# Segment sums of a state-space mixer as two fp32r products, with the steps split into a high and a low part

## The reference

```python
cs = jnp.cumsum(dt * a.reshape(g, r), axis=2)
seg = cs[:, :, :, None] - cs[:, :, None, :]
decay_in = jnp.exp(jnp.where(lower, seg, -jnp.inf))
cb = jnp.einsum('bcqgn,bcsgn->bcqsg', cm, bm)
m = cb[..., None] * decay_in * dt[:, :, None]
y_diag = jnp.einsum('bcqsgr,bcsgrp->bcqgrp', m, x)
```

## Time and profile before

| | us |
|---|---|
| median of 3 runs | 3049.22 |
| lowest, highest | 3045.48, 3049.49 |
| the profiled execution | 3067.35 |
| its span, first to last instruction | 3065.7 |
| TensorE busy | 2827.2 (92%) |
| VectorE busy | 2144.5 (70%) |
| ScalarE busy | 1532.5 (50%) |
| GpSimd busy | 188.3 (6%) |
| mean granted TensorE clock | 0.962 of 2.4 GHz |

### The profile page before, as it was taken

The page is one execution under the profiler, slowest core; times in us unless marked ns, Lnnn a source line. Parts: engine busy times, 40 slices in busy tenths (PEclk is TensorE's granted clock), DMA queues, the critical chain, the costliest instruction groups (busy, mean ns, idle before and its releaser), DMA issues. The chain is left out here.

```text
span 3065.7 us, 50810 instructions
## 1 busy us (share of the span) xinstructions
PE 2827.2 (92%) x17878; PEld 2422.8 (79%) x17878; DVE 2144.5 (70%) x4117; ACT 1532.5 (50%) x2880; POOL 188.3 (6%) x180
## 2 busy tenths in 40 slices
PE   5999688899997993999999999999999999999993
PEld 4999455566665873999999999999999999999992
DVE  3565755666665448787788788788788778778773
ACT  4443444454444332565555555555655555555552
POOL 0000011011110001000000000000000000000001
PEclk8999888999999995999999999999999999999996
DMA  6111310121222434776787777677677677677754
GB/s 250 65 66 55 116 36 30 43 100 57 92 83 100 163 126 165 243 241 224 244 254 225 233 253 230 229 253 238 222 251 242 217 249 250 222 245 241 230 189 175
DMA packets 359718, 547.40 MB, mean 179 GB/s; under 512 B 14784, under 2 KB 287936, under 8 KB 359616
## 3 DMA queue, kind: packets, MB, share of 16 engines
q1 hardware_dynamic: 350720, 514.59, 49.2%
q0 software_dynamic: 8896, 31.46, 4.5%
HBM read 493.51 MB, written 52.49 MB: 178 GB/s over the span
## 5 line engine op out<-in xcount | busy, mean ns | idle before, releaser
L2578 PE MATMUL banks<-rowsT_parts,weights_high 128*128 128x384 f32 x4096 | 1184.7, 361 | 11.0 <-DVE hidden_parts L2507 7.1
L2579 PE MATMUL banks<-rowsT_parts,weights_low 128*128 128x192 f32 x4096 | 1026.4, 251 | 0.0
L2578 PEld LDWEIGHTS banks<-rowsT_parts,weights_high 128*128 128x128 f32 x4096 | 770.1, 188 | 19.9 <-DVE hidden_parts L2507 9.8
L2579 PEld LDWEIGHTS banks<-rowsT_parts,weights_low 128*128 128x128 f32 x4096 | 783.5, 191 | 1.4
L2444 DVE TENSOR_TENSOR weights_low<-keys_or_w_out,weights_high 128x1024 fp32r<-128x1024 f32 x512 | 603.0, 1216 | 1.4 <-ACT weights_high L2384 1.4
L2384 ACT ACTIVATE weights_high<-keys_or_w_out 128x1024 fp32r<-128x1024 f32 x512 | 523.8, 1049 | 39.6 <-PEq L2182 39.6
L2589 PE MATMUL banks<-weights_high,hidden_parts 128*128 128x512 f32 x1536 | 435.7, 392 | 0.0
L2494 DVE TENSOR_TENSOR h_or_keys_or_sums<-banks,h_or_keys_or_sums 128x192 f32<-128x192 f32 x512 | 181.2, 354 | 330.8 <-ACT h_or_keys_or_sums L2410 330.8
L2410 ACT ACTIVATE h_or_keys_or_sums<-banks 128x192 f32<-128x192 f32 x512 | 165.7, 324 | 460.2 <-PE banks L2579 456.4
L2589 PEld LDWEIGHTS banks<-weights_high,hidden_parts 128*128 128x128 f32 x1536 | 283.4, 188 | 69.8
L2589 PE MATMUL banks<-weights_low,hidden_parts 128*128 128x512 f32 (+1 forms) x1024 | 319.4, 393 | 0.0
(11 more groups left out here) (298 smaller groups left out, 3552.7 us busy)
## 6 DMA issues: line engine op xcount, KB each, us to landing
keys_or_w_out<-w_gate SPq DMA_DIRECT2D x128, 1024.0 KB, 5.1
keys_or_w_out<-w_up SPq DMA_DIRECT2D x128, 1024.0 KB, 6.8
slab_down<-w_down SPq DMA_DIRECT2D x128, 1024.0 KB, 4.8
arena_attend<-w_ada SPq DMA_DIRECT2D x8, 2048.0 KB, 7.5
arena_attend<-ssd_tiles SPq DMA_DIRECT2D x12, 992.0 KB, 9.0
arena_inputs<-w_ada SPq DMA_DIRECT2D x4, 2048.0 KB, 11.7
ssd_tiles<-arena_inputs SPq DMA_DIRECT2D x24, 256.0 KB, 2.0
mixed<-arena_attend SPq DMA_DIRECT2D x12, 512.0 KB, 2.9
```

Source lines behind the costliest of these rows:

```text
L2578: nc.tensor.matmul(out[:, 0:2 * CT], w_hi[:, u, block], x[:, k, :], start=k == 0, stop=False)
L2579: mm = nc.tensor.matmul(out[:, 0:CT], w_lo[:, u, block], x[:, k, 0:CT], start=False, stop=k == KD - 1)
```

## The change

Four things:

- The steps of a tile, `dta`, are split on VectorE (`steps`, new): `step_hi` is a cast to fp32r of [128, 16], `step_lo` the difference. This stands in slot h = 2 for the tile that follows, and in front of the first tile's spreads.
- `r_sum` has a part of each kind and is fp32r. VectorE makes both forward parts, [128, 8, 128] each, in slot h = 3, after the rotation; the spread in slot h = 6 goes. GpSimd makes both backward parts, and waits for `steps_done` in place of the tile's load.
- A segment product is two fp32r products into the same bank, with the triangles copied to fp32r once (`turns_r`).
- Places in the arena move to make room, and `eps_done` becomes part of `cleared`.

```diff
-    r_sum = A.at(A_R, 2, NS, P)
+    r_sum = core.once("decay_steps", [P, 2, 2, NS, P], F32R)
+    turns_r = core.once("triangles", [P, 2, P], F32R)
+    step_hi = core.once("steps_high", [P, 2, 16], F32R)
+    step_lo = core.once("steps_low", [P, 2, 16])
...
         def _(pool):
             def terms(g, j):
 
-                wait_apart(pool, tile_in[j], turn_of(g, j) + 16, pool_turns)
+                wait_apart(pool, steps_done, g + 1, pool_turns)
                 wait_apart(pool, seg_mm, g * 4, pool_turns)
-                nc.gpsimd.tensor_tensor(r_sum[:, 1], core.masks[:, M_GE, :].unsqueeze(1).broadcast_to([P, NS, P]),
-                                        dta[j][:, 8:16].unsqueeze(2).broadcast_to([P, NS, P]),
-                                        ALU.mult).then_inc(terms_b, 1)
+                for part, steps in enumerate((step_hi[:].bitcast(F32), step_lo[:])):
+                    ins = nc.gpsimd.tensor_tensor(r_sum[:, part, 1], core.masks[:, M_GE, :].unsqueeze(1).broadcast_to([P, NS, P]),
+                                                  steps[:, j, 8:16].unsqueeze(2).broadcast_to([P, NS, P]), ALU.mult)
+                ins.then_inc(terms_b, 1)
...
-            def terms(g, j):
+            def steps(g, j):
 
                 dve.wait_ge(tile_in[j], turn_of(g, j) + 16)
+                if not early(g):
+                    dve.wait_ge(terms_b, g - 1)
+                nc.vector.tensor_copy(step_hi[:, j], dta[j]).then_inc(steps_high, 1)
+                dve.wait_ge(steps_high, g + 3)
+                nc.vector.tensor_tensor(step_lo[:, j], dta[j], step_hi[:, j].bitcast(F32), ALU.subtract).then_inc(steps_done, 1)
+
+            def terms(g, j, part):
+                dve.wait_ge(steps_done, g + 1)
                 dve.wait_ge(seg_mm, g * 4)
-                nc.vector.tensor_tensor(r_sum[:, 0], core.masks[:, M_LE, :].unsqueeze(1).broadcast_to([P, NS, P]),
-                                        dta[j][:, 0:8].unsqueeze(2).broadcast_to([P, NS, P]),
-                                        ALU.mult).then_inc(terms_f, 1)
+                nc.vector.tensor_tensor(r_sum[:, part, 0], core.masks[:, M_LE, :].unsqueeze(1).broadcast_to([P, NS, P]),
+                                        (step_hi[:].bitcast(F32), step_lo[:])[part][:, j, 0:8].unsqueeze(2)
+                                        .broadcast_to([P, NS, P]), ALU.mult).then_inc(terms_f, 1)
...
+                    for d in range(2):
+                        nc.vector.tensor_copy(turns_r[:, d], core.masks[:, (M_GT, M_LT)[d], :]).then_inc(steps_high, 1)
                     keys_dve(dve, lambda t: front(t + 3, lo, 0, 0))
-                    terms(lo, 0)
+                    steps(lo, 0)
+                    for part in range(2):
+                        terms(lo, 0, part)
...
-                    if follows and h == 6:
-                        terms(g + 1, 1 - j)
...
                     if follows and h < 6:
                         front(h + 1, g + 1, place, 1 - j)
+                    if follows and h == 2:
+                        steps(g + 1, 1 - j)
+                    if follows and h == 3:
+                        for part in range(2):
+                            terms(g + 1, 1 - j, part)
...
             def seg(g, p, behind):
 
                 d, grp = divmod(p, 2)
-                pe.wait_ge((terms_f, terms_b)[d], g + 1)
+                pe.wait_ge((terms_f, terms_b)[d], g + 1 if d else g * 2 + 2)
                 if p:
                     pe.wait_ge(e_done, g * 4 + p)
                 elif behind is not None:
                     pe.wait_ge(y_mixed, behind + 1)
-                nc.tensor.matmul(b_y, core.masks[:, (M_GT, M_LT)[d], :],
-                                 r_sum[:, d, 4 * grp:4 * grp + 4, :].rearrange("p h q -> p (h q)"),
-                                 start=True, stop=True).then_inc(seg_mm, 1)
+                for part in range(2):
+                    mm = nc.tensor.matmul(b_y, turns_r[:, d, :],
+                                          r_sum[:, part, d, 4 * grp:4 * grp + 4, :].rearrange("p h q -> p (h q)"),
+                                          start=part == 0, stop=part == 1)
+                mm.then_inc(seg_mm, 1)
```

More of the change, by code:

```diff
@@ L181, in small, with once @@
         return self.stage.enter_context(self.nc.sbuf_tensor(name, shape, dtype))
-    def once(self, name, shape):
+    def once(self, name, shape, dtype=F32):
         if name not in self.kept:
-            self.kept[name] = self.small(name, shape)
+            self.kept[name] = self.small(name, shape, dtype)
         return self.kept[name]
@@ L228, in at @@
         return v.rearrange(f"p ({' '.join(names)}) -> p {' '.join(names)}", **dict(zip(names, dims)))
-ARENA = 48256
-A_NAT = 25984
-A_SLAB, A_MODT = 25984, 30080
+ARENA = 44032
+A_NAT = 24576
+A_SLAB, A_MODT = 24576, 28672
 SLABS = 4
@@ L334, in inputs @@
     heads = lambda t: t.rearrange("p (h e) -> p h e", h=NS)
-    consts_in, silu_c, cleared, eps_done = sem("consts_in"), sem("silu_c"), sem("mod_cleared"), sem("eps_set")
+    consts_in, silu_c, cleared = sem("consts_in"), sem("silu_c"), sem("eps_and_mod_cleared")
     slab_in = [sem(f"ada_slab_in{s}") for s in range(SLABS)]
@@ L624, in take_x @@
                     nc.scalar.activation(xnat[t], b_S1, ACT.Copy).then_inc(xnat_done, 1)
-            act.wait_ge(eps_done, 1)
+            act.wait_ge(cleared, 1)
             stats(0)
@@ L689, in _ @@
             nc.vector.memset(core.eps[:, 0:1], EPS)
-            nc.vector.memset(core.eps[:, 1:2], 1.0).then_inc(eps_done, 1)
+            nc.vector.memset(core.eps[:, 1:2], 1.0).then_inc(cleared, 1)
             nc.vector.memset(b_X[0][:, 0:P], 0.0)
@@ L1085, in _ @@
             pe.wait_ge(silu_c, 1)
-            pe.wait_ge(cleared, 1)
+            pe.wait_ge(cleared, 2)
             for s in range(SLABS):
@@ L1118, in _ @@
             chunk_state(NT - 1)
[L1121 to L1129, removed]
+A_KT, A_WUQ, A_V = 0, 8192, 9728
+A_P, A_PT = 13824, 15872
+A_KN, A_QN = 17920, 42496
+A_CN, A_CT2 = 19456, 20224
+A_MIXT = 20992
+A_OT, A_ROT = 23040, 23552
+A_QT, A_O = 28800, 30848
+A_E, A_XDT, A_Y, A_CBM = 32896, 34944, 35968, 38016
+A_REC, A_JUNKM = 38528, 24064
 A_KROT = A_NAT + NT * (NAT - QL)
@@ L1312, in mixers @@
         sem(n) for n in ("off_mm", "off_done", "diag_mm", "y_order", "y_gated", "y_sumsq", "y_rstd", "y_normed", "y_turned", "y_mixed"))
+    steps_high, steps_done = sem("triangles_and_steps_high"), sem("steps_split")
     pool_turns, dve_turns = sem("mix_pool_turns"), sem("mix_dve_turns")
@@ L1872, in first @@
                     pe.wait_ge(sem(name), hi)
+                if not r:
+                    pe.wait_ge(steps_high, 2)
                 scores(lo, 0, 0)
```

## The result

The changed kernel takes 3030.08 us (median of 3 runs, 3026.71 to 3030.28) against 3049.22 before, a ratio of 0.9938 with a 95% interval of 0.9915 to 0.996. Timed again, five rounds beside the experiments, it took 3028.04 us against 3048.08, 0.9939 [0.9925, 0.9953].

The account below looks back on a forecast made before the run. TensorE was taken to bound a sample tile. Sample products -11.5, prompt products -6.5, removed slot -1.8, prompt tile ends -3.0 and start +3 gave -19.8 us, from 3049.22 to 3029.4 us, range 3018 to 3042.

Parts of the forecast that it names:

- The case that I called likeliest: Whole kernel: the forecast of 3029.4 us, chance 0.58, with its own range of 3021 to 3037 us.
- The removed slot: Seventh slot (h = 6): without its spread, 0.25 us saved in seven sample tiles, 1.8 us in all.
- The products: Segment products: each 0.405 us shorter at full clock, 1.44 us per sample tile, 11.5 us over eight.
- the work in slots three to five: Sample tiles: new VectorE and GpSimd work uses 5.0 of 5.1 us of cover, costed at nothing, bound 0 to 2 us.
- I give all four: 1.62 us: Prompt tiles: all four segment products' savings come back, 1.62 us per tile, 6.5 us over four tiles.
- the overrun of VectorE's queue: First prompt tile: some 3.5 us of cover for 5 us of work, 1.5 us charged, cancelling that tile's gain at its end.
- rival (a): VectorE's queue overruns its cover by about 1 us in 11 tiles, or the start costs 8.7; 3040 us, chance 0.24.
- The prompt tile's last wait: End of a prompt tile: TensorE's 1.68 us wait for the probability copy falls to 0.69, 3.0 us over three tiles.
- The start: First prompt tile: idle gap in the keys goes, -4 us; collision before the first maximum costs 7; net +3.
- (b): State product is held by GpSimd too, costing 18 us in all; 3047 us, no change, chance 0.08.
- (c): GpSimd is slow writing fp32r, 3.4 us per product instead of 2.04; 3057 us, slower, chance 0.08.
- (d): Two fp32r segment products cost what one fp32 did, leaving only ends and start, -2; 3047 us, chance 0.02.

Follow-up runs that it names:

- e2: Kernel before the change with only the forward spread moved from slot h = 6 to h = 3, fp32 products kept; 3039.7 us, ratio 0.9967.
- e6: Changed kernel with a third GpSimd product per tile, the low backward part spread twice into the same place; 3037.52 us, ratio 0.9965.
- e7: Changed kernel with one forward spread, the high part, used for both forward products, low part left out; 3046.83 us, ratio 0.9992.
- after: The changed kernel itself; 3030.08 us, ratio 0.9938 to the kernel before the change.
- e8: Changed kernel with the cast and high forward spread in slot h = 2, subtraction and low spread left where they were; 3027.9 us, ratio 0.9937.
- before: The kernel without the change; 3049.22 us, and 3048.08 us when timed again in five rounds.
- e4: Kernel before the change with GpSimd's first spread held until the prompt keys are done; 3044.05 us, ratio 0.9984.
- e10: Kernel before the change, unchanged, profiled again and timed against itself; span 3045.6 us, ratio 0.9995.
- e3: Changed kernel with GpSimd's first pair of the prompt held until the first maximum; 3029.62 us, ratio 0.9934.
- e11: Changed kernel, unchanged, timed again in five rounds beside the experiments and profiled; 3028.04 us, ratio 0.9939.
- e5: Changed kernel with each segment product made only once, from the high part, all spreads still made; 3023.05 us, ratio 0.9919.
- e1: Changed kernel with both forward spreads put back in front of the last maximum, slot h = 6; 3066.33 us, ratio 1.0053.

## Why the prediction was right

Forecast 3029.4 us, measured 3030.08 and, in five rounds, 3028.04. The case that I called likeliest came true, but three of its terms came out right by errors of opposite sign: a product's, the prompt tile's and the start's.

**Sample tiles: right.** -13.3 us forecast, -12.8 in the balance. The removed slot gave 0.26 us (e2: 48.2), as counted. The products gave 1.3 (48.2 to 46.87) of 1.44. The saving of 0.405 us each was right as a sum only: a pair takes 0.55 us to the next instruction, not 0.455 as in the row of nothing but such products, and the transposes ahead of it give back 0.08 us that I had not counted. The row from the fourth prompt tile to the first sample tile adds 1.9 to the balance of -12.8, with the clock in it, as said above; the six tiles at full clock carry the finding (-9.6 of -10.1). That the work in slots three to five is covered held as well, with more margin than I had counted (e6, e7).

**Prompt tiles: the sum nearly right, the terms not.** The forecast was 2.62 us per tile. At full clock, in the middle tile, it is 0.9 (35.0 to 34.1). The move gave 1.1 (e2). From e2 to after the products took another 1.2 us off TensorE's busy time (30.27 to 29.07), and nothing was left of it: 1.2 came back as the wait for the exponential and 0.5 as a wait for ScalarE's reading of the segment sums (L1500), while another wait fell by 0.4. The step that failed is "I give all four: 1.62 us". I had charged the overrun of VectorE's queue to the first prompt tile alone, at 1.5 us, though the second and the third have the same short heads; it shows in these too, and e8 takes it away. This is rival (a), true in the prompt tiles only. What brought the sum back is the clock: tiles two and four of before had stretches at 1.2 GHz (0.94 and 0.93), and after has 0.95 and 1.00 there, so that these two gave 5.8 us together. I had left such stretches for the range. The figure of -6.7 us holds luck as well as mechanism: the clock of these tiles repeats (e4 as e10, e3 and e11 as after), which speaks for the change as its cause, but nothing in my sum had foreseen it, and in the execution of the prediction it was another.

**The prompt tile's last wait: right size, wrong place.** I had read the 1.68 us before the eighth slot's transposes as that which falls to 0.69. It stayed (1.65 in after); the exponential's wait ahead of it went.

**The start: the net right, both terms too large.** Forecast +3 with the first tile's products at -1.6; measured +1.9 against +1.4. The wait before the first transposes grew from 0.95 to 5.85 us, by 4.9, where I had charged 7. The sum that I gave for the most doesn't add up as written: 0.4, two spreads and two GpSimd products are 6.9 us. 5.7 is the sum with one spread, and that is the right addition, since the kernel before had the other one there. The keys took 5.7 us less than in the execution of the prediction, but only 2.5 to 3.1 less than in e10, where the gap that I read as 3.72 us is 2.80; I had taken 4. From the first transposes to the first y it is 0.5 to 0.7 us less, where the first tile's products were to give 1.62. e3 shows that a shorter gap there is no gain by itself, since the clock takes it back behind; e4, that the edit to the keys alone keeps 2.3 us.

**The rivals.** (b) fell: L1630 took 0.68 us beside GpSimd's spread, and TensorE waited 0.41 us as before. The rule of the Trainium skill, "SBUF — State Buffer", section "Who interferes with whom", holds here on both sides: this instruction with one input in PSUM was free, those with two inputs in SBUF (L1135, L1603, L1137) were held. The norm L1667, a tensor and one number per partition, was held too (2.13 us), which that rule would lay to a 2-port mode; no run here separates the two. (c) fell: GpSimd takes 1.90 us with an fp32r output. (d) fell by the rows at 692.71 and by e5. The side of slower had a case after all, but not one of mine: the same two spreads left in the emptied slot (e1).

## What to carry to other kernels

Before two long vector instructions are put side by side, look at what the other engine that shares SBUF has due in that slot, in each kind of tile: what is covered in the long tile may be one for one in the short one. Follow the cover to the instruction of the bounding engine that takes up the result, not to the first engine behind. And compare stretches at equal clock: a term taken from a tile with half-clock stretches can be out by more than itself, and a wait that is saved ahead of such a stretch can be lost in it (e3, e8).

## What the runs showed of the hardware

- Two fp32r products of 512 columns cost 0.455 us in a run of such products and 0.55 when other work follows each pair (0.32 for a single one, e5); one fp32 product costs 0.86, and the transposes ahead of it start 0.49 us before it instead of 0.41.
- GpSimd and VectorE, both with two inputs in SBUF, alternate instruction by instruction when both have a queue: 2.65, 2.92 and 2.87 us for what takes 1.90, 1.22 and 1.90 alone. A short instruction pays the other's rest too (0.28 became 1.98 in e6, at 718.12).
- One program has executions of about 3045 us and, more seldom, of 3061 to 3067 (3 of 23 in one series). The two profiled ones, 3045.6 and 3065.7, differ most in three prompt tiles, with a clock of 0.94, 1.00 and 0.93 in the one and 0.83 in the other.
- A start with 3.4 us less of waiting before its first transposes took 3.0 us more up to the first y: it ran at a clock of 0.80 instead of 0.91 (e3).
- In e7 the stages behind the edit took 20 us longer, from a cause that is not shown: marks at the stage's end tell more than the total.
